# Two decoder blocks in one launch: the last residual added by a transfer in DRAM instead of by two engines in SBUF

## The chip, the cores and the metric

The kernel runs on one core of a Trainium2 chip. The metric is the device time of one execution in microseconds (us). Before the change three runs gave 1675.19, 1676.03 and 1676.67 us, a median of 1676.03 us. One more execution was taken with the hardware profiler; all durations and moments below come from it, and moments count from the start of its span.

## The reference, cut to what matters

Two transformer blocks are applied one after the other to a sequence of 512 tokens of width 1024. Only the last step is touched. The second block ends with

```
y = conv_ffn(h, ...)                       # up projection, gated, w_down_2
x = x + g2 * rms_norm(y, post_ffn_g)       # the output
```

x is the residual stream as it stands after the second block's token mixer, y the product of the second feed-forward network, and rms_norm divides each token by the root of the mean of its squares. In the kernel channels lie on the 128 partitions: x and y are held as 128 x 8 x 512 floats, k = 0..7 counts blocks of 128 channels, and the output has the same layout, 2 MB in all.

## The kernel before

The work is written out by hand for the five engines; each runs its own list in program order and meets the others at semaphores. A list of "units" streams the weights: SP loads a unit into one of two slots of `raw` (`load_unit`, L673), ScalarE rounds it to `w_hi` (L1431), GpSimd subtracts for `w_lo` (L724, `split_lo`), and TensorE multiplies each weight tile three times (high by high, high by low, low by high; L896 for whole tiles, L889 for the half tiles of a last unit). SP may load a unit once GpSimd has split the unit two places ahead of it. SP's loop `for u in units` at L693 holds all loads, with one other transfer in it, the 2 MB reload of x at L697.

Around the start of the second feed-forward network, `cross5` in GpSimd's list (L797) adds the mixer's normed product to x; the semaphore `x_pool` counts these 16 additions. From there on x isn't written until the end. GpSimd makes them before it splits the weights of the unit FU (0,1), and so on in the order of the units.

The end is `cross6`. The 512 tokens are split into two halves of 256 (`half_cols`, h = 0 and 1). For each half DVE adds the last products into `ysum` (`evict_half`, L2362), ScalarE squares them, DVE sums the squares (`add_square_of`, L2279), TensorE sums over the channels, ScalarE takes the root (L1630), DVE inverts it (`invert_of`, L2285), and TensorE spreads it over the partitions into the banks auxA (h = 0) and auxB (h = 1). Then `output` (L2366) goes over the 8 blocks of each half: `scale_y` (L2289, 128 x 256 elements) makes ysum the normed, gated product, and x + ysum is formed in x, for blocks 0, 2, 4 by DVE itself (L2375) and for the other five by GpSimd (L795, told by `z_mul`). SP stores each finished block of 128 KB (L703), 16 stores in `OUT_ORDER`, and waits for all of them.

Of the kernel before, what the change touches and what calls it, by code (L numbers as in the profile page):

```python
# [9 lines left out]
ALU = mybir.AluOpType  # L10
# [6 lines left out]
KD = D_MODEL // P  # L17
# [326 lines left out]
def build(nc, stream, w_ada, w_ada2, x_in, params_in, consts_in, out):  # L344
# [32 lines left out]
    with ExitStack() as ctx:  # L377
        def alloc(stack, name, shape, dt=F32):
            return stack.enter_context(nc.sbuf_tensor(name, [P] + list(shape), dt))
# [8 lines left out]
        x = alloc(ctx, "x", [KD, SEQ])  # L388
# [69 lines left out]
        with ExitStack() as s7:  # L458
            s7.enter_context(nc.sbuf_tensor("skip7", [P, 2 * G2_HALF * SEQ + SEQ], F32))
            ysum = alloc(s7, "ysum", [KD, SEQ])  # L460
# [4 lines left out]
        def sem(name):  # L465
            return ctx.enter_context(nc.semaphore(name))
# [8 lines left out]
        x_first = [sem(f"x_first{i}") for i in range(4)]  # L475
# [86 lines left out]
        crossing = {unit_at["OUT"][3]: 1, unit_at["DN"][15]: 2, unit_at["WO"][3]: 5, unit_at["FD"][15]: 6}  # L562
        ORDER = {1: 0, 2: 1, 5: 2}
        acc4, squares = og[:, 0, :], [og[:, 1, :], og[:, 2, :], og[:, 3, :], hm[:, 0, :]]
        OUT_ORDER = (1, 3, 0, 5, 7, 2, 6, 4)
        BY_DVE = (0, 2, 4)
        BY_POOL = tuple(k for k in OUT_ORDER if k not in BY_DVE)
        half_cols = (slice(0, SEQ // 2), slice(SEQ // 2, SEQ))
        root, r_col = small[:, 32:36], small[:, 36:40]
        first_unit_after = {0: 0, 1: unit_at["UP"][0], 2: unit_at["KV"][0], 5: unit_at["FU"][0]}  # L570
# [29 lines left out]
        def squared(i):  # L600

            return KD * (i if i < 5 else i - 1)

        def added(k, h):

            if k in BY_POOL:
                return x_pool, 2 * KD + len(BY_POOL) * h + BY_POOL.index(k) + 1
            return x_ready, 4 * KD + len(BY_DVE) * h + BY_DVE.index(k) + 1


        turn_of = {}
        for g in range(GROUPS):
# [58 lines left out]
        @block.sync  # L671
        def _(sp):
            def load_unit(u):  # L673
                s = u.n % 2
                if u.n >= 2:
                    sp.wait_ge(lo_done, pieces_before[u.n - 1])
                k = u.kn * u.cols
                sp.dma_start(raw[:, s, 0:k], stream[u.n, :, 0:k]).then_inc(raw_in[s], 16)

            sp.dma_start(par[:, :], params_in).then_inc(par_in, 16)  # L680
            sp.dma_start(con[:, :], consts_in).then_inc(par_in, 16)
            for q in range(4):
                sp.dma_start(x[:, 2 * q:2 * q + 2, :], x_in[:, 2 * q:2 * q + 2, :]).then_inc(x_first[q], 16)
            load_unit(units[0])
            for s in (1, 0):
                for k in range(KD):
                    if s == 0:
                        sp.wait_ge(first_in[k], 16)
                    sp.dma_start(ada_first[:, KD * s + k, :],
                                 w_ada[P * k:P * (k + 1), ADA_COLS * s:ADA_COLS * (s + 1)]).then_inc(first_in[k], 16)  # L690
            load_unit(units[1])
            load_unit(units[2])
            for u in units:  # L693
                if u.name == "OUT" and u.tag == 2:

                    sp.wait_ge(mx_lo, KD)
                    sp.dma_start(x[:, :, :], x_in).then_inc(x_back, 16)  # L697
                if u.n >= 3:
                    load_unit(u)
            for h in range(2):  # L700
                for k in OUT_ORDER:
                    sp.wait_ge(*added(k, h))
                    sp.dma_start(out[:, k, half_cols[h]], x[:, k, half_cols[h]]).then_inc(out_done, 16)  # L703
            sp.wait_ge(out_done, 32 * KD)

        @block.gpsimd
        def _(pool):
# [85 lines left out]
            def add_residual(k, h):  # L793
                cols = half_cols[h]
                nc.gpsimd.tensor_tensor(x[:, k, cols], x[:, k, cols], ysum[:, k, cols], ALU.add).then_inc(x_pool, 1)  # L795
# [6 lines left out]
                        add_residual(k, h)  # L802

            def cross6():
                for h in range(2):
                    for n, k in enumerate(BY_POOL):
                        pool.wait_ge(z_mul, 2 * KD + len(BY_POOL) * h + n + 1)
                        add_residual(k, h)

            link(nc.gpsimd.memset(small[:, 40:44], -0.5))  # L810
            split_lo(units[0])
            for u in units:
# [11 lines left out]
                run(early.get((u.n + 1, 0), []))  # L824
                run(end[u.n])
            cross6()

        @block.tensor
# [1161 lines left out]
        def _(dve):  # L1990
            chain = [0]

            def link(ins):
                chain[0] += 1
                ins.then_inc(dve_chain, 1)
                dve.wait_ge(dve_chain, chain[0])

            stt, tt, ts = nc.vector.scalar_tensor_tensor, nc.vector.tensor_tensor, nc.vector.tensor_scalar

            def full(stage, k):  # L2000
                b, use = bank_use[stage][k]
                dve.wait_ge(aux_full[b], use + 1)
                return aux[b], aux_free[b]

            def tile(j):
                dve.wait_ge(main_full[j % 4], j // 4 + 1)
                return main[j % 4], main_free[j % 4]
# [264 lines left out]
            def add_square_of(i, k, h):  # L2272
                cols = half_cols[h]
                if h:
                    dve.wait_ge(norm_sq, squared(i) + k + 1)
                else:
                    dve.wait_ge(sq_half, 2 * (i // 2) + k - KD + 3)
                to = (acc4 if i == 4 else rstd[:, :])[:, cols]
                link(tt(to, to, tmp[:, k % 2, cols], ALU.add))  # L2279
                dve.sem_inc(norm_add if h else add_half, 1)  # L2280

            def invert_of(i, h):
                c = slice(2 * h, 2 * h + 2)
                dve.wait_ge(rt_half, 2 * (i - 2) + h + 1)
                nc.vector.reciprocal(r_col[:, c], root[:, c]).then_inc(root_half, 1)  # L2285

            def scale_y(m_, k, h, r):
                cols = half_cols[h]
                return stt(ysum[:, k, cols], ysum[:, k, cols], mul[:, m_, k:k + 1], r[:, cols], ALU.mult, ALU.mult)  # L2289
# [67 lines left out]
            def cross6(u):  # L2357

                def evict_half(k, h):
                    bank, free = tile(u.job0 + 2 * h + k - (KD - 2))  # L2360
                    cols = half_cols[h]
                    link(tt(ysum[:, k, cols], ysum[:, k, cols], bank[:, 0:SEQ // 2], ALU.add))  # L2362
                    dve.sem_inc(free, 1)
                    dve.sem_inc(ysum_ready if h else y_half, 1)

                def output(h, ks):  # L2366
                    cols = half_cols[h]
                    r, free = full(("cross", 6), 2 * h + 1)
                    for k in ks:
                        ins = scale_y(5, k, h, r)  # L2370
                        if k in BY_POOL:
                            ins.then_inc(z_mul, 1)
                        else:
                            link(ins)
                            tt(x[:, k, cols], x[:, k, cols], ysum[:, k, cols], ALU.add).then_inc(x_ready, 1)  # L2375

                run(mid[u.n])
                dve.wait_ge(ysum_ready, 16)
                for k in (KD - 2, KD - 1):
                    evict_half(k, 0)  # L2380
                    add_square_of(6, k, 0)
                run(end[u.n])
                invert_of(6, 0)
                evict_half(KD - 2, 1)
                output(0, OUT_ORDER[:2])
                add_square_of(6, KD - 2, 1)
                evict_half(KD - 1, 1)
                output(0, OUT_ORDER[2:5])
                invert_of(6, 1)
                output(0, OUT_ORDER[5:7])  # L2390
                output(1, OUT_ORDER[:2])
                output(0, OUT_ORDER[7:])
                output(1, OUT_ORDER[2:])

            def cross(u, v, i):

# [374 lines left out]
            def run(steps):  # L2771
                for name, item in steps:
                    n = count.get(name, 0)
                    count[name] = n + 1
                    if name in stages:
                        stages[name](item, n)
# [114 lines left out]
```

## Time and profile before

| what | value |
|---|---|
| median of three runs | 1676.03 us |
| profiled execution, its own time | 1676.24 us |
| its span, first to last instruction | 1674.4 us |
| TensorE busy, share of the span | 1629.1 us, 97% |
| mean granted clock of TensorE, share of full | 0.991 |
| GpSimd, ScalarE, VectorE (DVE) busy | 814.1, 679.9, 893.3 us |

The profiled execution is longer than its span by 1.84 us, which lie before the first or after the last instruction. PE is TensorE, POOL is GpSimd, SPq the queue of transfers that SP issues. A line such as L2289 is a line of the kernel's file. The tables of rows give a moment, then a duration, then what ran; a row with "x2" joins two instructions that follow each other.

### The profile page before, as it was taken

To read this page: it belongs to the slowest core of one execution; us is meant where nothing else is said; L and a number is where in the kernel's file an instruction comes from. 1 tells how busy PE (TensorE), PEld (TensorE's weight loads), DVE (VectorE), ACT (ScalarE), POOL (GpSimd) and SP (SyncE) were. 2 spreads that over 40 slices of the span, in tenths; PEclk is the share of its full clock that TensorE was granted. 3 is DMA by queue.
4 is the path that set the end of the run, shared out by engine and by line. 5 is a ranking of instruction groups with operands and counts; after the bars stand their busy time and mean duration, and the time that the engine had idled before them with its cause. 6 is when DMAs were issued, how large, how long until landed. Compare 5 with 4: busy or idle time off the path is not lost.

```text
span 1674.4 us, 21912 instructions
## 1 busy us (share of the span) xinstructions
PE 1629.1 (97%) x8026; PEld 1359.9 (81%) x8026; DVE 893.3 (53%) x1226; ACT 679.9 (41%) x1103; POOL 814.1 (49%) x665
## 2 busy tenths in 40 slices
PE   5999999999999999999999999999999999999997
PEld 5787888888887888888888889778878888888886
DVE  7687555556675355644345534876467655024324
ACT  3554544444333223542124323455655543334431
POOL 1374746556455554544454444432357354544443
PEclk7999999999999999999999999999999999999999
DMA  8221122222235445244545541221112242232221
GB/s 325 75 76 66 65 91 82 76 76 93 84 120 194 165 137 214 102 151 176 191 163 199 201 151 61 79 92 51 51 51 101 101 149 81 96 115 101 85 89 66
DMA packets 36825, 194.40 MB, mean 116 GB/s; under 512 B 4080, under 2 KB 6384, under 8 KB 21488
## 3 DMA queue, kind: packets, MB, share of 16 engines
q1 hardware_dynamic: 25200, 151.06, 24.9%
q10 hardware_dynamic: 11520, 41.95, 7.4%
q8 instruction: 65, 1.06, 0.2%
q14 instruction: 40, 0.33, 0.1%
HBM read 190.90 MB, written 2.10 MB: 115 GB/s over the span
## 4 chain that ended last, share of the span: by engine, by line
PE 84%; DVE 9%; ACT 3%; issue 2%; DMA 1%; POOL 1%; ACTq 0%; DVEq 0%; SPq 0%; POOLq 0%
PE main L896 62%; PE main L892 7%; PE main L889 2%; PE auxD L1207 2%; DMA x<-x_in 1%; PE main L996 1%; DVE tmp L2591 1%; PE auxD L1272 1%; ACT w_hi L1431 1%; DVE ysum L2289 1%; PE auxC L1200 1%; PE auxB L1194 1%; DVE ada_first L2187 0%; PE auxB L1246 0%; DVE x L2270 0%
## 5 line engine op out<-in xcount | busy, mean ns | idle before, releaser
L724 POOL TENSOR_TENSOR w_lo<-raw,w_hi 128x512 fp32r<-128x512 f32 x521 | 697.0, 1369 | 694.0 <-ACT w_hi L1431 690.1
L896 PE MATMUL main<-h_hi,w_hi 128*128 128x512 f32 (+1 forms) x1016 | 399.2, 393 | 1.5 <-DVEq L2086 1.5
L896 PE MATMUL main<-h_hi,w_lo 128*128 128x512 f32 (+1 forms) x1016 | 396.4, 390 | 0.0
L896 PE MATMUL main<-h_lo,w_hi 128*128 128x512 f32 (+1 forms) x1016 | 396.3, 390 | 0.0
L1431 ACT ACTIVATE w_hi<-raw 128x1024 fp32r<-128x1024 f32 (+2 forms) x267 | 257.7, 1013 | 232.2 <-PE main L896 173.8
L896 PEld LDWEIGHTS main<-h_hi,w_hi 128*128 128x128 f32 (+1 forms) x1016 | 190.6, 188 | 42.0 <-issue 2.7
L896 PEld LDWEIGHTS main<-h_hi,w_lo 128*128 128x128 f32 (+1 forms) x1016 | 190.5, 187 | 40.9
L896 PEld LDWEIGHTS main<-h_lo,w_hi 128*128 128x128 f32 (+1 forms) x1016 | 190.5, 188 | 39.5
L2162 DVE SCALAR_TENSOR_TENSOR tmp<-main,par,tmp 128x511 f32<-128x511 f32 x88 | 65.9, 749 | 162.1 <-ACT tmp L1545 160.3
L2187 DVE SCALAR_TENSOR_TENSOR ada_acc<-ada_raw,cs,ada_acc 128x1024 f32<-128x1024 f32 x70 | 106.5, 1522 | 33.5 <-DMA ada_raw<-w_ada 24.0
L892 PE MATMUL main<-w_hi,h_hi 128*128 128x512 f32 x224 | 90.1, 402 | 0.0
L892 PE MATMUL main<-w_lo,h_hi 128*128 128x512 f32 x224 | 88.0, 393 | 2.1 <-POOL w_lo L724 2.0
L892 PE MATMUL main<-w_hi,h_lo 128*128 128x512 f32 x224 | 87.5, 391 | 0.0
L896 PE MATMUL main<-f_hi,w_hi 128*128 128x512 f32 x224 | 87.4, 390 | 0.0
L896 PE MATMUL main<-f_hi,w_lo 128*128 128x512 f32 x224 | 87.2, 389 | 0.0
L896 PE MATMUL main<-f_lo,w_hi 128*128 128x512 f32 x224 | 87.2, 389 | 0.0
L2019 DVE SCALAR_TENSOR_TENSOR tmp<-main,half,tmp 128x511 f32<-128x511 f32 (+2 forms) x96 | 71.8, 748 | 15.3 <-ACT tmp L1454 12.3
L2113 DVE TENSOR_TENSOR tmp<-tmp 128x512 f32<-128x512 f32 x32 | 32.4, 1013 | 74.2 <-ACT f_hi L1515 73.6
L896 PE MATMUL main<-g_hi,w_hi 128*128 128x512 f32 x154 | 59.9, 389 | 0.0
L896 PE MATMUL main<-g_lo,w_hi 128*128 128x512 f32 x154 | 59.9, 389 | 0.0
L896 PE MATMUL main<-g_hi,w_lo 128*128 128x512 f32 x154 | 59.9, 389 | 0.0
L1511 ACT ACTIVATE tmp<-main 128x512 f32<-128x512 f32 x32 | 19.1, 597 | 91.6 <-PE main L896 89.5
(524 smaller groups left out, 2862.8 us busy)
## 6 DMA issues: line engine op xcount, KB each, us to landing
raw<-stream SPq DMA_DIRECT2D x118, 1024.0 KB, 4.8
ada_raw<-w_ada ACTq DMA_DIRECT2D x80, 512.0 KB, 4.4
ada_first<-w_ada SPq DMA_DIRECT2D x16, 512.0 KB, 10.0
raw<-stream SPq DMA_DIRECT2D x8, 768.0 KB, 4.2
raw<-stream SPq DMA_DIRECT2D x8, 640.0 KB, 3.9
x<-x_in SPq DMA_DIRECT2D x4, 512.0 KB, 7.4
x<-x_in SPq DMA_DIRECT2D x1, 2048.0 KB, 10.5
out<-x SPq DMA_DIRECT2D x16, 128.0 KB, 1.8
```

The costliest lines, as they stand in the source:

```text
L724: nc.gpsimd.tensor_tensor(lo[:, a:b], raw[:, s, a:b], hi[:, a:b], ALU.subtract).then_inc(lo_done, 1)
L889: ins = nc.tensor.matmul(bank[:, 0:SEQ // 2], w[:, k, chunk(t % 2)], a[:, ka_, half_cols[t // 2]], start=start, stop=stop)
L892: ins = nc.tensor.matmul(bank[:, 0:u.cols], a[:, ka_, chunk(t)], w[:, k, :], start=start, stop=stop)
L896: ins = nc.tensor.matmul(bank[0:n, :], w[:, k, col:col + n], a[:, ka_, :], start=start, stop=stop)
L996: ins = nc.tensor.matmul(bank[:, half_cols[h]], w[:, k, chunk(t)], a[:, k, half_cols[h]], start=start, stop=stop)
L1207: ins = nc.tensor.matmul(bank[:, HD * k:HD * (k + 1)], decay[:, k, :], xdt[:, 0, HD * k:HD * (k + 1)], start=True, stop=True)
L1431: run_act(hi[:, a:b], raw[:, s, a:b], ACT.Copy).then_inc(hi_done, 1)
L1511: link(run_act(tmp[:, n % 2, :], bank[:, :], ACT.Relu))
L2019: ins = stt(acc[:, d:SEQ], bank[:, 0:SEQ - d], w[:, 3 - d:4 - d], acc[:, d:SEQ], ALU.mult, ALU.add)
L2113: link(tt(tmp[:, 2 + n % 2, :], tmp[:, n % 2, :], tmp[:, n % 2, :], ALU.mult))
L2162: link(stt(acc[:, d:SEQ], bank[:, 0:SEQ - d], wt, acc[:, d:SEQ], ALU.mult, ALU.add))
L2187: link(stt(acc, src, c, acc, ALU.mult, ALU.add))
```

## The change

Block two's residual x is stored whole to the output (one 2 MB transfer) from SP's loop, right behind the load of the unit FU (0,4), once `x_pool` tells that `cross5` is through. At the end nobody adds x: DVE only scales, all eight blocks of a half in plain order 0 to 7, with no instruction between the scales and no wait for its own last result. GpSimd, in place of its ten additions, issues six transfers that add a piece of ysum to what lies in the output (`accum_op=ALU.add`): two pieces of four blocks for the first half of the tokens, four pieces of two blocks for the second. In each piece a partition gives rows of 256 floats (1 KB), one for each block. SP's 16 stores are gone. SP waits for the 2 MB store and for the six pieces.

```
-        OUT_ORDER = (1, 3, 0, 5, 7, 2, 6, 4)
-        BY_DVE = (0, 2, 4)
-        BY_POOL = tuple(k for k in OUT_ORDER if k not in BY_DVE)
+        OUT_PARTS = ((0, 0, 4), (0, 4, 8), (1, 0, 2), (1, 2, 4), (1, 4, 6), (1, 6, 8))
...
                 if u.n >= 3:
                     load_unit(u)
-            for h in range(2):
-                for k in OUT_ORDER:
-                    sp.wait_ge(*added(k, h))
-                    sp.dma_start(out[:, k, half_cols[h]], x[:, k, half_cols[h]]).then_inc(out_done, 16)
-            sp.wait_ge(out_done, 32 * KD)
+                if u.name == "FU" and u.tag == (0, 4):
+                    sp.wait_ge(x_pool, 2 * KD)
+                    sp.dma_start(out, x[:, :, :]).then_inc(x_first[1], 16)
+            sp.wait_ge(x_first[1], 32)
+            sp.wait_ge(out_done, 16 * len(OUT_PARTS))
...
             def cross6():
-                for h in range(2):
-                    for n, k in enumerate(BY_POOL):
-                        pool.wait_ge(z_mul, 2 * KD + len(BY_POOL) * h + n + 1)
-                        add_residual(k, h)
+                pool.wait_ge(x_first[1], 32)
+                for h, a, b in OUT_PARTS:
+                    pool.wait_ge(z_mul, 2 * KD + KD * h + b)
+                    cols = half_cols[h]
+                    nc.gpsimd.dma_start(out[:, a:b, cols], ysum[:, a:b, cols], accum_op=ALU.add).then_inc(out_done, 16)
...
                     for k in ks:
-                        ins = scale_y(5, k, h, r)
-                        if k in BY_POOL:
-                            ins.then_inc(z_mul, 1)
-                        else:
-                            link(ins)
-                            tt(x[:, k, cols], x[:, k, cols], ysum[:, k, cols], ALU.add).then_inc(x_ready, 1)
+                        scale_y(5, k, h, r).then_inc(z_mul, 1)
...
-                output(0, OUT_ORDER[:2])
+                output(0, range(2))
                 add_square_of(6, KD - 2, 1)
                 evict_half(KD - 1, 1)
-                output(0, OUT_ORDER[2:5])
+                output(0, range(2, 5))
                 invert_of(6, 1)
-                output(0, OUT_ORDER[5:7])
-                output(1, OUT_ORDER[:2])
-                output(0, OUT_ORDER[7:])
-                output(1, OUT_ORDER[2:])
+                output(0, range(5, KD))
+                output(1, range(KD))
```

## Rows read from the trace of the kernel before

**Rows 1.** Page: span, busy time by engine, chain's shares by engine.
```profile
span 1674.4 us, 21912 instructions
...
PE 1629.1 (97%) x8026; PEld 1359.9 (81%) x8026; DVE 893.3 (53%) x1226; ACT 679.9 (41%) x1103; POOL 814.1 (49%) x665
...
PE 84%; DVE 9%; ACT 3%; issue 2%; DMA 1%; POOL 1%; ACTq 0%; DVEq 0%; SPq 0%; POOLq 0%
```

**Rows 2.** Chain of waits, last 15 us: start, duration, engine, tile, line.
```profile
1659.94 0.87 DVE ysum L2289 x2
1660.81 0.71 DVE rstd L2279
...
1662.32 0.49 DVE ysum L2289
...
1665.41 1.58 DVE ysum L2289 x4
...
1671.41 0.66 DVE x L2375
```

**Rows 3.** Groups by line and shape, 1653 to the end: busy us, mean ns.
```profile
L795 POOL TENSOR_TENSOR x<-x,ysum 128x256 f32<-128x256 f32 x10 | 7.4, 761 | 14.6 <-DVE ysum L2289 14.6
...
L2375 DVE TENSOR_TENSOR x<-x,ysum 128x256 f32<-128x256 f32 x6 | 3.9, 652 | 0.2
```

**Rows 4.** Timeline of the tail: start, duration, engine, line, operation.
```profile
1655.53 0.42 DVE L2279 TENSOR_TENSOR rstd<-rstd,tmp 128x256 f32<-128x256 f32 x1 [0.63 <-ACT tmp L1695]
...
1660.50 1.59 POOL L795 TENSOR_TENSOR x<-x,ysum 128x256 f32<-128x256 f32 x2 [10.69 <-DVE ysum L2289]
...
1663.48 0.26 ACT L1630 ACTIVATE small<-auxD,par 128x2 f32<-128x2 f32 x1 [0.80 <-PE auxD L1057]
...
1664.26 0.68 PE L962 MATMUL auxB<-con,small 128*128 128x128 f32 x4 [0.82 <-DVE small L2285]
```

**Rows 5.** The tile x in the tail: ns min/median/max, first and last start; time to landing.
```profile
L703 SPq DMA_DIRECT2D out<-x x16: 332/338/460, 1661.3 to 1672.2; - x16
L795 POOL TENSOR_TENSOR x<-x,ysum x10: 722/724/912, 1660.5 to 1671.1; 128x256 f32<-128x256 f32 x10
...
DMA to landing us min/median/max: 1.7/1.8/1.9
```

**Rows 6.** Transfers from 1661 to the end: packets, queue's share of 16 engines.
```profile
DMA packets 2304, 2.10 MB, mean 157 GB/s; under 512 B 256, under 2 KB 2304, under 8 KB 2304
...
q1 hardware_dynamic: 2304, 2.10, 44.8%
```

**Rows 7.** Transfers from 1671 to the end, 40 slices of 0.085 us: GB/s.
```profile
GB/s 0 0 241 373 386 374 157 72 253 386 386 326 133 0 0 0 0 0 0 133 337 386 386 253 49 193 361 386 386 193 24 0 0 0 0 0 0 0 0 0
```

**Rows 8.** Around the load of FU (0,4): its issue, ScalarE's use, TensorE's busy time.
```profile
1323.44 0.33 SPq L678 DMA_DIRECT2D raw<-stream  x1
...
1336.18 1.99 ACT L1431 ACTIVATE w_hi<-raw 128x1024 fp32r<-128x1024 f32 x2
...
1317.00:1337.00 20.00, 20.00 (x90) 16.57 (x89) 12.72 (x15) 9.66 (x13) 10.54 (x8) 1.00 0.37 134
```

**Rows 9.** Reload of x at 633: transfers 630 to 646, then busy time by engine.
```profile
x<-x_in SPq DMA_DIRECT2D x1, 2048.0 KB, 10.5
raw<-stream SPq DMA_DIRECT2D x2, 1024.0 KB, 11.2
...
633.00:645.00 12.00, 12.00 (x55) 9.94 (x54) 1.16 (x3) 1.26 (x2) 5.04 (x4) 1.00 0.94 356
```

**Rows 10.** Page: weight loads, KB each, median us from issue to landing.
```profile
raw<-stream SPq DMA_DIRECT2D x118, 1024.0 KB, 4.8
```

More of the change, by code:

```diff
@@ L602, in squared @@
             return KD * (i if i < 5 else i - 1)
-        def added(k, h):
-            if k in BY_POOL:
-                return x_pool, 2 * KD + len(BY_POOL) * h + BY_POOL.index(k) + 1
-            return x_ready, 4 * KD + len(BY_DVE) * h + BY_DVE.index(k) + 1
         turn_of = {}
@@ L2366, in output @@
                 def output(h, ks):
-                    cols = half_cols[h]
                     r, free = full(("cross", 6), 2 * h + 1)
                     for k in ks:
-                        ins = scale_y(5, k, h, r)
-                        if k in BY_POOL:
-                            ins.then_inc(z_mul, 1)
-                        else:
-                            link(ins)
-                            tt(x[:, k, cols], x[:, k, cols], ysum[:, k, cols], ALU.add).then_inc(x_ready, 1)
+                        scale_y(5, k, h, r).then_inc(z_mul, 1)
                 run(mid[u.n])
```

## The prediction

> **What bounds the kernel now.** I read the page first: TensorE is busy 97% of the span, and the chain that ended last runs 84% on it [rows 1]. The change adds nothing to TensorE and takes nothing from it, so it can act in two places only: where a 2 MB store enters the weight stream, and in the tail behind the last product. I then followed the chain of waits through its last 15 us. From 1659.94 on every piece of weight in it is a DVE instruction: scales of ysum (L2289), one sum of squares, additions into x (L2375), the last of which ends at 1671.41 + 0.66 = 1672.07 [rows 2]. The last store is issued at 1672.2 and lands about 1.8 us later, near 1674.0 [rows 5]; 0.4 us remain to the end of the span at 1674.4 [rows 1]. So the tail is DVE's work, then the landing of one store, and that landing is the moment whose shift I work out. The profiled execution took 1676.24 us, 1.84 over its span and 0.2 over the median of 1676.03; I add to 1676.24.
>
> **What it removes.** Six DVE additions at a mean of 652 ns, 3.9 us in all, stand on the chain [rows 3]; with them go about six gaps of 0.02, 0.1 us. GpSimd's ten additions, 7.4 us, lay beside DVE and were waiting for it [rows 3]; they cost nothing themselves, but DVE's sum of squares shows what they do to a neighbour: 0.42 us when GpSimd was idle, 0.71 on the chain when GpSimd added at 1660.50 [rows 2, 4]. I take 0.3 back there. The scales cost the same as before, 1.58 / 4 = 0.40 us each in a row of four [rows 2]. A gain has a check: the second half can't be scaled before its reciprocal is spread. ScalarE's root ended at 1663.74 and the spread at 1664.94 [rows 4]; both come 0.3 earlier with the sum of squares, and DVE now reaches its reciprocal first, which costs it about 0.3 of waiting. In sum DVE ends at 1672.07 - 3.9 - 0.1 - 0.3 + 0.3 = 1668.0, 4.0 us earlier.
>
> So the pieces become ready as follows. First half: two scales by 1660.81, two more from 1662.0, so blocks 0 to 3 at 1662.8; blocks 4 to 7 at 1664.8, which is 1668.0 less eight scales of 0.40. Second half, a pair each 0.80: 1665.6, 1666.4, 1667.2, 1668.0.
>
> **What it adds at the end: six adding transfers by GpSimd.** The trace of before holds no transfer issued by GpSimd and none that adds, so both of its parts are bounded.
>
> Issue. From below: SP issues one transfer in 0.34 us [rows 5]. From above: writing the descriptors of a piece takes GpSimd as long as the additions it replaces, 0.72 us for each 128 x 256 block at the median [rows 5], so 2.9 us for four blocks and 1.45 for two. I take 1.0 us for each piece, nearer the row for an issue than the row for arithmetic, because no data pass through GpSimd but rows of descriptors do.
>
> Movement. Each piece is rows of 1 KB, as the old stores were. Those kept 16 engines busy for 44.8% of 13.4 us = 6.0 us to move 2.10 MB, and each engine carried 2304 / 16 = 144 packets, so 42 ns for a packet [rows 6]; in the bursts they ran at 386 GB/s, which is the same number [rows 7]. From below: adding costs no more than storing, 42 ns a row. From above: fetching the old row, fetching the new one and writing the sum follow one another, three times 42, 126 ns. I take 84 ns: a row that is to be added to must come in too, so two rows enter an engine for each that leaves, and entering and leaving overlap as they do in a plain store. The fixed part is read from the last store: issued near 1672.2, the last burst of bytes begins in slice 24 or 25 of rows 7, near 1673.05, 0.85 us later [rows 7], and of its 1.8 us, 0.85 and 8 x 0.042 leave 0.6 for the end of landing.
>
> Sum. The first piece's bytes start at 1662.8 + 1.0 + 0.85 = 1664.65. Each engine has 128 rows in the six pieces, 128 x 0.084 = 10.75 us, and no gap opens between pieces: the second is there by 1664.8 + 1.85 = 1666.65, when the first still runs (32 rows, to 1667.3), the third by 1667.65, before 1670.0. So the bytes end at 1675.4 and land at 1676.0, against 1674.0 now: 2.0 us later. The 4.0 us that DVE gains are spent on engines that now carry the sum, and the end is set by 16 transfer engines where it was set by DVE. Predicted: 1676.24 + 2.0 = 1678.2 us.
>
> With a single term changed the sum gives: 42 ns a row, 1674.1 (the last piece is issued behind its predecessors by 1669.8 and lands 0.85 + 0.67 + 0.6 later, at 1671.9); 42 ns and an issue of 0.34, landing 1670.1, so 1672.3, the lowest; issue at 0.72 a block with 84 ns, last issue ends 1674.4, landing 1677.2, so 1679.4; 126 ns, 1683.6, the highest.
>
> **What it adds in the middle: a 2 MB store.** It stands in SP's queue behind the load of FU (0,4), issued at 1323.44 [rows 8]. Its wait for x_pool is long satisfied there, since that load itself waits for a split that GpSimd makes after the additions; behind it wait only the loads of later units, the next at 1331.9. The load it stands beside is used by ScalarE at 1336.18, 12.7 us after its issue, and lands in 4.8 us alone [rows 8, 10]. The trace has the like: the 2 MB reload of x at 633 took 10.5 us, two 1 MB loads beside it took 11.2 instead of 4.8, and TensorE was busy 12.00 of 12 us all the same [rows 9]. 11.2 is inside 12.7, TensorE is busy 20.00 of 20 here too [rows 8], and I cost the store at nothing. Without that cover it would cost what the load is late: behind the whole store it lands 4.8 + 10.5 = 15.3 after issue, 2.6 late, near 1680.8 in all.
>
> **A rule beside it.** The stores of before took 1.8 us from issue to landing for 128 KB [rows 5]. The Trainium skill (DMA: Bandwidth & Descriptors, "Anatomy of one DMA — SWDGE (gpsimd) path") puts a GpSimd-issued transfer at 2.0 us plus its bytes at 436 GB/s, and says that many descriptors can be written before their number costs anything. By it the last piece of 256 KB takes an estimated 2.6 us from 1668.0, lands at 1670.6, and the time would be 1672.8, inside the cheap rival below. The rule is for copies; no row here shows an adding one.
>
> **The rivals.**
> 1. The sum as above, 1678.2, own range 1676.2 to 1679.4 (some overlap of the two reads; a first issue that costs 0.7 more; the high bound of issue). Chance 0.37.
> 2. Adding is as cheap as storing. Then DVE's end plus one landing decides: 1674.1, or down to 1672.3 if issue is cheap too. For it: the stores ran at 386 GB/s in bursts with idle slices between [rows 7], so there is room. Against it: every old row must be fetched. Chance 0.24, of which 0.09 lies more than 0.2% below.
> 3. Slower: the transfer engines are the bound and an added row costs three passes, because the write can't start until both reads are in, or GpSimd's descriptors come at the pace of such rows. 1683.6. It decides from (1677.35 - 0.6 - 1664.65) / 128 = 95 ns a row, little above my 84. For it: eleven microseconds of back-to-back rows leave no slack to hide a longer one. Against it: plain reads and writes overlap today. Chance 0.34.
> 4. The store collides with the weights and TensorE waits: 1680.8. Against it stands the reload at 633 [rows 9]. Chance 0.05.
>
> **How the numbers follow.** 0.2% is 3.35 us, about what can be told from no change. Faster: 0.09, from rival 2's low end. Slower: 0.34 + 0.05 + 0.02 from the top of case 1, 0.41. Within: 0.50. The range holds case 1, most of rival 2 and rival 3 to a little past its price: 1672.8 to 1685.0. The likeliest case is case 1, 1678.2.
>
> **What would show it.** In the changed kernel DVE's last scale should end near 1668 with no additions on the chain, and GpSimd should show six issues of about 1 us each. The share of the transfer engines from 1665 to 1675 should be near 1, with about 10.75 us of busy time each, 84 ns a row; 42 would prove rival 2, 126 rival 3. The last piece should land about 8 us after DVE's end; if it lands within 4, the adding is not what sets the end. TensorE should be as busy as before from 1317 to 1350. The prediction is wrong if GpSimd's issue takes several microseconds a piece, so that its queue, not the engines, orders the end, or if TensorE shows a gap near 1336.

## The result and the profile after

The changed kernel took 1680.69 us at the median of its runs (1677.73 to 1682.81) against 1675.86 us, a ratio of 1.0029 with a 95% interval of 1.0019 to 1.0039: slower by 4.8 us, where 2.0 was forecast and 1678.2 us named. It lies inside the range of 1672.8 to 1685.0, 2.5 us over the likeliest case and 2.9 under rival 3's price. The profiled execution took 1681.76 us.

First the page of the changed kernel: span, the chain's shares, and the new queue. The 2.10 MB of the adding transfers appear as q0, 0.9% of the engines' time, and the bytes written to HBM have doubled. The second fence is the HBM line of the page before.

```profile
span 1679.9 us, 21889 instructions
...
q0 software_dynamic: 2144, 2.10, 0.9%
...
HBM read 190.90 MB, written 4.19 MB: 116 GB/s over the span
...
PE 85%; DVE 8%; ACT 3%; issue 2%; POOL 1%; DMA 0%; ACTq 0%; DVEq 0%; POOLq 0%; SPq 0%
```
```profile
HBM read 190.90 MB, written 2.10 MB: 115 GB/s over the span
```

The bytes read from HBM are the same in both, though the adding needs the 2.10 MB of old rows. The page's count doesn't hold that reading, so where and when the old rows are fetched is not seen in any view here.

The profiles differ by nearly 4 us before the tail (the last half-tile multiplication starts between 1657.65 and 1661.48), so I measure the tail by itself: from the start of the last half-tile multiplication to the end of the span. That start in the timeline of TensorE, before and after:

```profile
1660.69 0.28 PE L889 MATMUL main<-g_hi,w_lo 128*128 128x256 f32 x1
```
```profile
1661.48 0.28 PE L881 MATMUL main<-g_hi,w_lo 128*128 128x256 f32 x1
```

The tail grew from 1674.4 - 1660.69 = 13.71 to 1679.9 - 1661.48 = 18.42 us, by 4.71 of the 4.83 by which the median changed. The 0.79 us between the two starts is not the early store's: SP's load of FU (0,4) is 0.80 late already, at 1324.24 instead of 1323.44 [rows 8], ahead of the store. Here is that load and the store, and TensorE's time around it (the busy columns are PE, PEld, DVE, ACT, POOL), in the changed kernel:

```profile
1324.24 0.33 SPq L669 DMA_DIRECT2D raw<-stream  x1
1324.61 0.48 SPq L693 DMA_DIRECT2D out<-x  x1
...
1336.97 1.99 ACT L1423 ACTIVATE w_hi<-raw 128x1024 fp32r<-128x1024 f32 x2
```
```profile
1317.00:1337.00 20.00, 20.00 (x90) 16.55 (x89) 12.17 (x14) 9.66 (x14) 10.55 (x8) 1.00 0.56 206
```

ScalarE uses the weights 12.73 us after their load was issued, where it was 12.74, and TensorE has no gap.

Now the tail of the changed kernel: DVE's last runs of scales and GpSimd's six issues in the timeline, the first issue by itself, then the output's transfers (ns min/median/max, and from issue to landing over all seven, the early store among them).

```profile
1662.73 1.26 DVE L2281 SCALAR_TENSOR_TENSOR ysum<-ysum,mul,auxA 128x256 f32<-128x256 f32 x3 [0.24 <-DVE ysum L2354]
...
1664.25 7.74 POOL L800 DMA_DIRECT2D out<-ysum  x6 [13.67 <-DVE ysum L2281]
...
1665.43 3.21 DVE L2281 SCALAR_TENSOR_TENSOR ysum<-ysum,mul,auxB 128x256 f32<-128x256 f32 x8
```
```profile
1664.25 1.49 POOL L800 DMA_DIRECT2D out<-ysum  x1 [13.67 <-DVE ysum L2281]
```
```profile
L800 POOL DMA_DIRECT2D out<-ysum x6: 1282/1954/3057, 1664.2 to 1668.9; - x6
...
DMA to landing us min/median/max: 6.7/9.0/12.6
```

DVE's scales end at 1668.64, 3.4 us before where its additions ended (1672.07 [rows 2]), or 4.2 with the 0.79 taken off; but a piece lands 6.7 us or more after its issue where a plain block took 1.8 [rows 5]. The transfers of the changed kernel from 1660 to 1680, 40 slices of 0.5 us, share of the engines and GB/s:

```profile
DMA  0000000000008996999999999999999999996000
GB/s 0 0 0 0 0 0 0 0 0 0 0 0 29 72 76 90 178 195 195 197 176 166 186 182 195 197 197 197 195 197 197 197 197 191 199 195 98 6 0 0
...
q0 software_dynamic: 2144, 2.10, 72.1%
```

The start of the flow and its end in slices of 0.1 us, from 1665.5 and from 1676:

```profile
GB/s 0 0 0 0 0 0 0 0 72 72 72 82 82 51 72 61 72 82 92 72 92 41 92 92 133 154 154 205 174 205 174 205 225 195 174 164 205 215 195 195
```
```profile
GB/s 184 195 205 195 205 174 195 215 195 174 195 195 205 195 205 205 164 215 205 184 133 113 123 92 31 21 10 0 0 0 0 0 0 0 0 0 0 0 0 0
```

Bytes flow from about 1666.3 to 1678.6 without a pause, most of it at 195 to 197 GB/s: 16 engines x 1024 bytes / 196 GB/s = 84 ns a row, as in the sum. The engines set the end, 10 us after DVE's last scale. GpSimd's last issue is over at 1664.25 + 7.74 = 1671.99, and the rate stays the same for six us more. Two things were not in the sum: the first 2 us run at 29 to 90 GB/s, and the first byte is late. In two stretches (the last two columns are the engines' share and GB/s):

```profile
1666.50:1667.00 0.50, 0.00 (x0) 0.00 (x0) 0.50 (x3) 0.00 (x0) 0.50 (x2) 1.00 1.08 72
```
```profile
1672.00:1674.00 2.00, 0.00 (x0) 0.00 (x0) 0.00 (x0) 0.00 (x0) 0.00 (x0) 0.50 1.23 196
```

In the slow stretch the engines are recorded as busy too (1.08 here), so it is mostly the rows that take longer there, not the engines that stand without work. A share over 1 says that the records of an engine's packets overlap; so the recorded busy time, 72.1% of 20 us = 14.4 us for each engine, is more than the 10.75 us of the forecast, though the rate is the forecast's.

### The profile page after: what moved, and what is told of

Read it like the earlier page. It is cut to its first block, busy times and chain, and to the rows that moved or that the text cites. A ratio compares the mean times of both kernels' runs of the same rounds, so it can differ in the third digit from the quotient of the medians.

```text
span 1679.9 us, 21889 instructions
## 1 busy us (share of the span) xinstructions
PE 1630.3 (97%) x8026; PEld 1360.5 (81%) x8026; DVE 889.0 (53%) x1220; ACT 679.9 (40%) x1103; POOL 814.4 (48%) x661
## 4 chain that ended last, share of the span: by engine, by line
PE 85%; DVE 8%; ACT 3%; issue 2%; POOL 1%; DMA 0%; ACTq 0%; DVEq 0%; POOLq 0%; SPq 0%
PE main L888 64%; PE main L884 7%; PE main L881 3%; PE auxD L1199 2%; DVE ada_first L2179 1%; PE main L988 1%; DVE tmp L2575 1%; PE auxD L1264 1%; PE auxC L1192 1%; PE auxB L1186 1%; PE auxB L1238 0%; DVE x L2262 0%; ACT w_hi L1423 0%; DVE ysum L2281 0%; PE main L986 0%
## 5 line engine op out<-in xcount | busy, mean ns | idle before, releaser
L2011 DVE SCALAR_TENSOR_TENSOR tmp<-main,half,tmp 128x511 f32<-128x511 f32 (+2 forms) x96 | 71.8, 748 | 15.3 <-ACT tmp L1446 12.3
## 6 DMA issues: line engine op xcount, KB each, us to landing
out<-x SPq DMA_DIRECT2D x1, 2048.0 KB, 12.6
```

The source lines that it names most:

```text
L2011: ins = stt(acc[:, d:SEQ], bank[:, 0:SEQ - d], w[:, 3 - d:4 - d], acc[:, d:SEQ], ALU.mult, ALU.add)
```

## The experiments

Each was run beside the kernel before on the same chip, in three groups, in which the kernel before had medians of 1675.49 (e1 to e4), 1675.21 (e5 to e8) and 1675.75 us (e9, e10). The ratio is to the kernel before of the same group, so it need not follow from the two medians in the table, whose 1675.86 was taken beside the changed kernel. The tail is measured as above, from each one's profile, one execution; where nothing in the tail was changed (before, e2_store_only) it is 13.71 and 13.76.

| kernel | median us | ratio (95%) | tail us |
|---|---|---|---|
| before | 1675.86 | | 13.71 |
| changed | 1680.69 | 1.0029 (1.0019 to 1.0039) | 18.42 |
| e1_plain | 1672.27 | 0.9983 (0.9974 to 0.9992) | 11.39 |
| e2_store_only | 1676.09 | 1.0001 (0.9992 to 1.0009) | 13.76 |
| e3_early | 1679.51 | 1.0027 (1.0017 to 1.0037) | 18.61 |
| e4_hybrid | 1675.11 | 1.0003 (0.9994 to 1.0012) | 14.89 |
| e5_wide | 1680.54 | 1.0033 (1.0021 to 1.0045) | 19.75 |
| e6_late_adds | 1676.07 | 1.0004 (0.9995 to 1.0012) | 14.22 |
| e7_eight | 1676.70 | 1.0009 (1.0000 to 1.0017) | 15.54 |
| e8_control | 1674.81 | 1.0001 (0.9993 to 1.0010) | 13.76 |
| e9_warm | 1679.31 | 1.0017 (1.0007 to 1.0026) | 18.29 |

**Is it the adding, or GpSimd's issuing?** e1_plain takes only the adding out of the changed kernel:

```
-  nc.gpsimd.dma_start(out[:, a:b, cols], ysum[:, a:b, cols], accum_op=ALU.add).then_inc(out_done, 16)
+  nc.gpsimd.dma_start(out[:, a:b, cols], ysum[:, a:b, cols]).then_inc(out_done, 16)
```

> The changed kernel with its six GpSimd transfers as plain stores of ysum: the residual is left out of the output, so the time is read for the transfers alone. Theory 1, the transfer engines set the end because an added row costs 84 ns where a stored one costs 42: rows fall back to about 42 ns, the end follows DVE again, 1672 to 1675 us, 5 to 8 less than the changed kernel. Theory 2, GpSimd's writing of descriptors paces the end: the six issues take the same, the time stays within 1 us of the changed kernel's, about 1680. Theory 3, a slow first stretch (about 75 GB/s for 1.7 us) belongs to transfers issued by GpSimd: it shows here too; if it belongs to adding, it is gone.

Measured: 8.4 us under the changed kernel by the medians, 0.17% under the kernel before. Its transfers from 1660 to 1680, and its issues:

```profile
GB/s 0 0 0 0 0 0 393 442 230 418 434 279 434 410 303 385 410 57 0 0 0 16 0 0 0 0 0 0 0 0 0 0 0 0 0 0 0 0 0 0
DMA packets 609, 2.11 MB, mean 105 GB/s; under 512 B 96, under 2 KB 96, under 8 KB 608
```
```profile
L800 POOL DMA_DIRECT2D out<-ysum x6: 710/719/956, 1661.5 to 1666.2; - x6
...
DMA to landing us min/median/max: 3.1/3.3/12.1
```

The same bytes, pieces and queue flow at up to 442 GB/s, with 393 in the first slice, and the engines wait for DVE between pieces. So theory 1 stands, and the slow first stretch belongs to adding (theory 3). For theory 2 this run alone isn't enough, since GpSimd issues a plain piece in 0.71 us and adding raises that to 1.28 at the least. But in the changed kernel the flow outlasts the last issue by over six us, and in e5_wide below the issues are over at 1666.90 and bytes flow until 1676: so it falls. One difference I had not foreseen, and which e5_wide takes up: the plain pieces travel in about 512 data packets, 4 KB each, the added ones in about 2048 of 1 KB (the rest, under 512 B, are 96 in both).

**Does the early store cost anything?** e2_store_only adds it to the kernel before:

```
+                if u.name == "FU" and u.tag == (0, 4):
+                    sp.wait_ge(x_pool, 2 * KD)
+                    sp.dma_start(out, x[:, :, :]).then_inc(x_first[1], 16)
+            sp.wait_ge(x_first[1], 32)
```

> The kernel before with the 2 MB store of x behind the load of FU (0,4) and nothing else changed (the last stores overwrite it). Theory 1: hidden, within 0.5 us of the kernel before, TensorE busy throughout. Theory 4, the store delays weights or what follows: 0.8 us or more over the kernel before, with a gap on TensorE near 1336.

Measured: a ratio of 1.0001 and the same tail; TensorE was busy 20.00 of 20 us beside it. Its transfers and the busy row:

```profile
L702 SPq DMA_DIRECT2D out<-x x1: 432/432/432, 1323.8 to 1323.8; - x1
```
```profile
1317.00:1337.00 20.00, 20.00 (x90) 16.57 (x89) 12.70 (x15) 9.66 (x13) 10.56 (x8) 1.00 0.62 226
```

The store is hidden; theory 4 and the prediction's rival 4 fall.

**Does an earlier start help?** e3_early cuts the pieces otherwise:

```
-        OUT_PARTS = ((0, 0, 4), (0, 4, 8), (1, 0, 2), (1, 2, 4), (1, 4, 6), (1, 6, 8))
+        OUT_PARTS = ((0, 0, 2), (0, 2, 5), (0, 5, 8), (1, 0, 3), (1, 3, 6), (1, 6, 8))
```

> The changed kernel with its six pieces cut 2, 3, 3 blocks in the first half and 3, 3, 2 in the second. The first piece is ready about 2 us earlier (after the two scales ahead of the sum of squares); same rows, same number of pieces. Theory 1, the engines run without a gap from the first byte: the end comes 1.5 to 2.5 us earlier than in the changed kernel, about 1678. Rival, what counts is a fixed time from DVE's last scale to the landing of the last piece: no change, about 1680.5.

Measured: 1679.51 us, tail 18.61: no gain that the tail shows. Its transfers from 1660 to 1680:

```profile
GB/s 0 0 0 53 121 143 164 100 57 104 170 201 168 156 178 180 137 102 86 107 125 170 197 195 193 199 201 195 188 150 107 37 12 0 0 0 16 0 0 0
```

Bytes do start earlier, near 1661.6 with the last multiplication at 1658.89: 2.7 us behind it, where the changed kernel's start 4.8 behind it. But the flow isn't steady: there are stretches at 53 to 143 GB/s at the start, 57 to 104 from 1663.5 to 1665, and 86 to 137 from 1668 to 1670.5. They give the two us back. So the slow stretch isn't only one of the first bytes, "128 rows at 84 ns after the first byte" is a lower bound, and theory 1's forecast of mine missed. Its rival has the number, but not a fixed time: the span ends 11.4 us after DVE's last scale here, 11.3 in the changed kernel and 12.6 in e5_wide. What slows the flow in between stays open.

**Do fewer added rows pay?** e4_hybrid adds four blocks by transfer and leaves twelve to the engines; its core:

```
+        BY_DMA = 4
+        BY_DVE = ((0, 6), (1, 1), (1, 4), (1, 7))
...
+                pool.wait_ge(z_mul, 2 * KD + BY_DMA)
+                cols = half_cols[0]
+                nc.gpsimd.dma_start(out[:, 0:BY_DMA, cols], ysum[:, 0:BY_DMA, cols], accum_op=ALU.add).then_inc(out_done, 16)
```

> Only the first four blocks of the first half are added by one GpSimd transfer (and only these are stored early, 512 KB); of the other twelve DVE adds four and GpSimd eight, stored by SP as before. Theory 1, adding transfers are slow but hidden while DVE still works: 32 rows an engine, 2.7 us, land before the last store; DVE loses two additions, so 1 to 2 us under the kernel before, about 1674.5. Theory 2, GpSimd's issuing costs what it takes from GpSimd's own additions: its queue is 1.5 to 3 us late and the end is at or over the kernel before, 1676 to 1678.

Measured: 1.0003, no gain; the tail is 1.2 us longer. The timeline of its DVE shows where the two spared additions went: the four that are left cost 0.95 us three times and once 1.92, 4.77 in all, where six cost 3.9 before (a mean of 652 ns [rows 3]). GpSimd isn't late, as theory 2 has it: it waits for DVE's scales before its last additions (the last line).

```profile
1662.57 1.92 DVE L2382 TENSOR_TENSOR x<-x,ysum 128x256 f32<-128x256 f32 x1
...
1665.70 0.95 DVE L2382 TENSOR_TENSOR x<-x,ysum 128x256 f32<-128x256 f32 x1
...
1667.86 0.95 DVE L2382 TENSOR_TENSOR x<-x,ysum 128x256 f32<-128x256 f32 x1
...
1670.02 0.95 DVE L2382 TENSOR_TENSOR x<-x,ysum 128x256 f32<-128x256 f32 x1
```
```profile
1669.28 1.41 POOL L799 TENSOR_TENSOR x<-x,ysum 128x256 f32<-128x256 f32 x2 [0.75 <-DVE ysum L2296]
```

e6_late_adds moves them behind the scales, e7_eight adds the whole first half by transfer, e8_control has no adding transfer at all:

```
e6:  +        BY_DVE = ((1, 5), (1, 6), (1, 7))
     +                for h, k in BY_DVE:
     +                    cols = half_cols[h]
     +                    tt(x[:, k, cols], x[:, k, cols], ysum[:, k, cols], ALU.add).then_inc(x_ready, 1)
e7:  +        BY_DMA = 8
     +        BY_DVE = ((1, 6), (1, 7))
e8:  +        OUT_LIST = [(h, k) for h in range(2) for k in range(KD)]     # all sixteen added by the engines
```

> As e4_hybrid (one adding transfer for four blocks), but GpSimd adds nine blocks and DVE only the last three, after all its scales, so that GpSimd doesn't wait for DVE between its additions. If e4_hybrid gained nothing because DVE's additions in between (0.95 to 1.92 us each) held back its scales and GpSimd with them, both engines end near 1669, about 2 us under the kernel before: 1673 to 1674.5. If the transfer engines held the last store back in e4_hybrid, no change from it: about 1675.

> As e6_late_adds with all eight blocks of the first half added by two transfers; GpSimd adds six blocks, DVE two. Theory 1 in doses: 64 rows at 84 ns and 64 at 42 are 8.1 us for each engine from about 1663, so the engines end near 1672 and it is 1 us or more slower than e6_late_adds though its engines add less: 1674.5 to 1676.5. Rival, what is spared on GpSimd and DVE decides: 0.5 to 1 us faster than e6_late_adds.

> e6_late_adds without any adding transfer and without the early store: blocks in plain order, GpSimd adds thirteen, DVE the last three after all its scales. GpSimd needs 13 x 0.72 = 9.4 us from about 1660.5. If the adding transfer is what helps in e6_late_adds, this is 1 us or more behind it, 1674.5 to 1676; if the order of DVE's work is what helps, it is as fast: 1673 to 1674.5.

Measured: 1.0004, 1.0009 and 1.0001. e6_late_adds missed its forecast, and the additions into x show why. First e6_late_adds (GpSimd's and DVE's in ns min/median/max, GpSimd's in the timeline, DVE's first in the chain of waits, and the adding transfer's us to landing), then DVE's in e8_control, and DVE's and GpSimd's in e7_eight:

```profile
L799 POOL TENSOR_TENSOR x<-x,ysum x9: 1172/1202/1239, 1663.6 to 1669.0; 128x256 f32<-128x256 f32 x9
L2400 DVE TENSOR_TENSOR x<-x,ysum x3: 411/412/2866, 1667.6 to 1670.8; 128x256 f32<-128x256 f32 x3
...
1663.57 6.64 POOL L799 TENSOR_TENSOR x<-x,ysum 128x256 f32<-128x256 f32 x9
...
1667.64 2.87 DVE x L2400
...
out<-ysum POOLq DMA_DIRECT2D x1, 512.0 KB, 6.9
```
```profile
L2391 DVE TENSOR_TENSOR x<-x,ysum x3: 841/937/939, 1667.8 to 1669.4; 128x256 f32<-128x256 f32 x3
```
```profile
L2401 DVE TENSOR_TENSOR x<-x,ysum x2: 410/1563/2716, 1668.6 to 1671.2; 128x256 f32<-128x256 f32 x2
...
1666.40 4.61 POOL L799 TENSOR_TENSOR x<-x,ysum 128x256 f32<-128x256 f32 x6
...
1668.59 3.05 DVE L2401 TENSOR_TENSOR x<-x,ysum 128x256 f32<-128x256 f32 x2
```

In e6_late_adds DVE's first addition took 2.87 us. It ended at 1670.51, 0.30 after GpSimd's last addition (1663.57 + 6.64 = 1670.21), and the two behind it took 0.41 each. In e7_eight the first took 2.72 and ended 0.30 after GpSimd's last as well. The 1.92 us of e4_hybrid came beside a pair of GpSimd's additions in the same way, ending 0.29 us after them. In e8_control, without an adding transfer, each took 0.84 to 0.94 beside GpSimd's. In the slow cases GpSimd's own additions are recorded at 1.2 us and overlap; what brings that about stays open.

With no, four and eight blocks added by transfer the tail is 13.76, 14.22 and 15.54 us. That is the order of theory 1's dose, but only e7_eight shows the transfers at work: its last addition ends at 1668.59 + 3.05 = 1671.64 and bytes flow for 4 us more. In e6_late_adds the adding transfer, issued at 1662.57, has landed 6.9 us later, before DVE's first addition is over; there it is DVE that is late. In the medians e7_eight lies 0.6 us over e6_late_adds, less than the 1 us that was forecast (1.3 in the tail), and e8_control 1.3 under it, so the adding transfer didn't help; the intervals of the three ratios overlap. The transfers of e7_eight from 1660 to 1680:

```profile
GB/s 0 0 0 0 0 0 0 0 0 0 0 0 49 74 92 113 186 197 197 197 162 211 231 221 219 238 262 336 379 381 336 127 4 0 0 0 0 0 0 0
```

None of these beats the kernel before.

**By the row or by the byte?** e5_wide issues four pieces whose data lie in runs of 4 KB:

```
-        OUT_PARTS = ((0, 0, 4), (0, 4, 8), (1, 0, 2), (1, 2, 4), (1, 4, 6), (1, 6, 8))
+        OUT_PARTS = ((0, 2), (2, 4), (4, 6), (6, 8))
...
+                    nc.gpsimd.dma_start(out[:, a:b, :], ysum[:, a:b, :], accum_op=ALU.add).then_inc(out_done, 16)
```

> The changed kernel with four pieces of two whole blocks, all 512 tokens, issued as the second half's scales end: a partition's data of a piece is then 4 KB in one run instead of rows of 1 KB. All pieces become ready about 3 us later than the changed kernel's first. Theory 1a, an added byte costs twice a stored one whatever the row: about 196 GB/s again, 10.7 us from about 1668.5, the end 3 us or more later than the changed kernel's, 1682 to 1685. Theory 1b, each added row costs a fixed time and long rows make it cheap: toward 386 GB/s, 1675 to 1678.

Measured: 1680.54 us, 1.3 us longer in the tail than the changed kernel, not 3: its bytes start 2 us later behind the last multiplication, but flow for 11.5 us instead of 12.3. The rate is what matters. GpSimd's four issues, and the transfers from 1660 to 1680:

```profile
1663.13 3.77 POOL L799 DMA_DIRECT2D out<-ysum  x4 [16.36 <-DVE ysum L2280]
```
```profile
GB/s 0 0 0 0 0 0 0 0 0 131 49 90 115 229 197 205 213 164 221 213 197 213 205 229 213 197 205 213 221 221 188 57 8 0 0 0 0 16 0 0
DMA packets 577, 2.11 MB, mean 105 GB/s; under 512 B 64, under 2 KB 64, under 8 KB 576
```

A quarter of the packets, and still 197 to 229 GB/s for most of the flow, about 210 in the mean. So it is mostly by the byte, theory 1a; the 1 KB rows cost less than a tenth. Its packets have the size of e1_plain's, 4 KB, so the packets' size is not what makes adding half as fast as storing.

**Why twice, and why a slow start?** e9_warm makes one small adding transfer early, and e10_sbuf adds into x in SBUF:

```
e9:  +                nc.gpsimd.dma_start(out[:, 0, 0:16], nothing, accum_op=ALU.add).then_inc(out_done, 16)
     +                pool.wait_ge(out_done, 16)
e10: -                    nc.gpsimd.dma_start(out[:, a:b, cols], ysum[:, a:b, cols], accum_op=ALU.add).then_inc(out_done, 16)
     +                    nc.gpsimd.dma_start(x[:, a:b, cols], ysum[:, a:b, cols], accum_op=ALU.add).then_inc(out_done, 16)
```

> The changed kernel with one more adding transfer from GpSimd near 1650, 16 zeros for each partition added to the output, and waited for before the pieces. If the slow first stretch (about 75 to 115 GB/s for 1.7 us in every kernel with adding transfers, and not with plain ones) is that of a first use, it is gone: bytes run near 196 GB/s from the start and the end comes 1 to 1.5 us earlier than in the changed kernel. If it is a ramp of adding transfers, it stays and the time is the changed kernel's.

> The six adding transfers with x in SBUF as their target instead of the output in HBM; no early store, and one 2 MB store at the end, so the time itself says nothing of the change (about 12 us more). Read for the rate. If an added byte costs twice a stored one because two rows enter an engine for each that leaves, wherever they lie, the rate is near 196 GB/s again. If the cost is that of reading the old row from HBM, it is above 300 GB/s, without the slow first stretch.

The small adding transfer of e9_warm, its transfers from 1660 to 1680, and those of e10_sbuf from 1660 to 1682 (slices of 0.55 us):

```profile
1648.78 1.07 POOL L797 DMA_DIRECT2D out<-small  x1
```
```profile
GB/s 0 0 0 0 0 0 0 0 29 94 90 96 180 197 197 180 137 164 203 199 199 193 197 197 193 199 193 197 199 195 197 190 76 8 0 0 0 16 0 0
```
```profile
GB/s 0 0 0 0 0 0 101 197 197 201 199 173 192 203 201 194 190 194 184 197 184 190 201 194 197 186 37 0 30 447 477 477 477 477 477 477 447 30 0 0
```

e9_warm keeps the slow stretch (29 to 96 GB/s) and the tail (18.29 us), so it is not a first use; its median lies 1.4 us under the changed kernel's, of which the tail accounts for 0.1, and I don't count the rest. e10_sbuf (1683.98 us, its time says nothing) runs at much the same rate, 173 to 203 GB/s, with both operands in SBUF, and so from its second slice; the plain store that follows goes at 477. So the half rate goes with the adding, wherever the old data lie; the slow stretch needs the output in HBM as the target. What in HBM makes it slow stays open. Why adding halves the rate is not shown either: two rows that enter for each that leaves would do it, and so would an addition that takes as long as a move, and no run tells the two apart.

## Why the prediction was right, and where its size was off

- DVE's end: forecast 1668.0, found 1668.64, less the 0.79 of shift 1667.85. The six additions are gone and the sum of squares takes 0.42, as priced; the wait for the reciprocal is 0.19 where 0.3 was. e1_plain shows what this is worth where nothing else takes over: 2.3 us of tail, and rival 2 was priced at 2.1.
- The early store: priced at nothing, measured at nothing (e2_store_only).
- The row: 84 ns by the rate, found 84. This is the term between the two bounds of 42 and 126, and it decided which case came; the value was right, while its reason, two rows in for each one out, is not shown. Rival 3's 126 ns are not seen.
- What failed is "the first piece's bytes start at 1664.65" and the flat rate behind it. The four scales are done at about 1663.6 - 0.79 = 1662.8, as forecast; GpSimd's issue starts at 1663.46, 0.66 later, which I had at zero; it then takes 1.49 us, not 1.0, and the bytes begin 0.55 behind it, not 0.85, near 1666.3 - 0.79 = 1665.5: 0.85 late. They flow for 12.3 us, not 10.75, which costs 1.55. Of this 1.0 us is lost by 1668.0, when 133 KB have moved where the flat rate moves 333; the rest goes in dips to 166 to 186 GB/s and at the end. From the end of the bytes to the end of the span 1.3 us pass, not 1.0. In sum 2.0 + 0.85 + 1.55 + 0.3 = 4.7, against 4.71 measured.
- The six issues took 1.28 to 3.06 us, not about 1. They didn't order the end, since bytes flowed at the same rate for six us behind the last of them.
- One of the sums with a single term changed is off: with 42 ns and an issue of 0.34, sixteen rows of the last piece make 0.67, as in the sum ahead of it, so it lands at 1670.5 and the lowest price is 1672.7, not 1672.3. Rival 2's low end moves with it and is still more than 0.2% below.
- Within or slower: the sum stood 1.35 us under the bound of 0.2%, and the 0.41 given to slower is what came, but of it only the 0.02 from the top of case 1 had this mechanism. It was the likeliest case's path with a larger size: 1680.69 lies over that case's own range, which ended at 1679.4, and inside the whole range because this reached to rival 3's price. To that extent the range held by luck.
- The price of the Trainium skill (DMA: Bandwidth & Descriptors, "Anatomy of one DMA — SWDGE (gpsimd) path") for a GpSimd transfer, an estimated 1672.8 in all, is near what the plain pieces gave (1672.27 in e1_plain, where a piece took 3.1 us or more to land, not 2.6). It doesn't hold for adding ones: the first, of 512 KB and with no other ahead of it, took 6.7 us to land, twice the median of the plain ones (3.3).

## What to carry to other kernels

An adding transfer frees the engine that added, but its bytes pass at half the rate of a store, so count 84 ns for each KB and engine, as here, before you move additions there, and more for a slow start into HBM. It hides only while something else still runs for longer than those bytes take, and even then four hidden blocks gained nothing here (e4_hybrid, e6_late_adds); as the last step of a kernel it replaces a short chain of engine work by a longer one of bytes. Before believing a saving on one engine, ask which resource the work goes to, and run once with the work left out (here the plain store) to see how much there was to gain: 2.3 us of tail.

## What the runs showed of the hardware that was not expected

- Adding transfers run at 173 to 203 GB/s with the target in SBUF (e10_sbuf), at 195 to 197 for most of the flow into HBM, and there at 197 to 229 with runs of 4 KB (e5_wide); plain ones from GpSimd reach 442 (e1_plain).
- Adding into HBM ran at 29 to 131 GB/s in its first 2 us in the changed kernel, e5_wide, e7_eight and e9_warm, in the changed kernel with the engines busy for most of them. e3_early, with smaller pieces, began at 53 to 164 and had such stretches later too. Adding into SBUF had none.
- GpSimd's issue of an adding piece with rows of 1 KB took 1.28 to 1.49 us when its queue was free, of a plain one 0.71 to 0.96. The first began 0.66 us after the scale that released it.
- A 128 x 256 addition of DVE took 0.84 to 0.95 us beside GpSimd's additions in e8_control and e4_hybrid. In e6_late_adds and e7_eight the first took 2.87 and 2.72 and ended 0.30 us after GpSimd's last one; those behind it took 0.41. The cause is open.
